# A third projection tile opened beside the first two behind a norm, in other PSUM banks, with its weights' low part on GpSimd

## The chip, the cores and the metric

One NeuronCore of a Trainium2 chip runs the whole kernel. The metric is the device time of one execution in microseconds (us). A program of 1 core has one span; lower is better.

## What is computed

Two layers of a backbone for 512 latent tokens and 256 context tokens of width 1024. Each layer is a token mixer and a gated feed-forward; here layer 0 mixes with a gated linear recurrence and layer 1 with windowed attention. Cut to what matters for this change:

```python
for i in range(DEPTH):                         # 2 layers
    hl = modulate(rms_norm(xl, norm1_g[i]), sh1, sc1)      # latent tokens; hc for the context tokens
    oc, ol = mixer_i(hc, hl, ...)              # i = 0: hgrn2, i = 1: qkv projection, rotation, attention
    xl = xl + g1 * ol
    h = modulate(rms_norm(xl, norm2_g[i]), sh2, sc2)
    u, v = jnp.split(h @ w_up, 2, axis=-1)     # 2 x 2816 columns
    u = conv3x3_depthwise(u) + conv_b          # on the 8 x 64 grid (1 x 3 for the context tokens)
    xl = xl + g2 * ((gelu(u) * v) @ w_down)
return rms_norm(xl, final_norm_g)
```

In layer 0 the context tokens go the same way; in layer 1 they give keys and values alone.

## The kernel before, in words

**Layout.** Channels lie on the 128 partitions, tokens on the free axis: `X[128, 8, 768]`, eight chunks of 128 channels, with 256 context tokens (`CTX`) and 512 latent ones (`LAT`), 768 together (`TOK`).

**Tiles.** A tile is one block of 128 output channels of a weight matrix. Its 1024 x 128 weights stream through three buffers (`WR`, `NB = 3`), in one fixed order of tile numbers `t`. Every product is made of three fp32r matmuls: high weights by high input, high by low, low by high. ScalarE makes the high part (`WH`, `split_high`), VectorE the low part (`WL`, L1433, `split_low`), as `WR - WH`. The semaphore `w_hi_done` counts high parts, `w_split` low parts, `tile_done` finished tiles. SyncE loads tile t when `tile_done` has reached t - 2.

**PSUM.** There are four pairs of banks: `SLOT[0]` and `SLOT[1]` for tiles in turn, `MA` for sums and matmuls that only keep TensorE busy, and `MB` for other things (the spread row of the norm among them). `begin_tile(s)` waits for `w_split` and for `evacuated[s]`, which counts the tiles that were taken out of slot s.

**The norm and the first tiles.** Behind a norm (`norm_dve`, `norm_act`) the input arrives in eight chunks: VectorE multiplies X by the coefficients and the row in `MB` (`scaled`, L1570) into one of two buffers `NT`, ScalarE adds the shift and rounds to the high part `HH` (L1077), VectorE makes the low part `HL` (`low`, L1577, reads `NT` and `HH`) and raises `lo_ready`. `first_tiles` works on two tiles at once, one chunk behind the other: it waits for each chunk and does both tiles' matmuls of it (L447 to L449). After that `third_tile` and `full_tile` do one tile each (768 tokens: L458). Behind chunk 5 VectorE makes the low weights of the third tile.

**The first feed-forward.** Tiles are u0, v0, u1, v1, ...: an odd one of the pair is convolved, an even one is the gate. Tile 50 (`T_FF0`) is u0 in slot 0, tile 51 is v0 in slot 1, tile 52 is u1, tile 53 is v1. ScalarE copies u0 to the padded grid `UP` (L1266, L1268) and scales it into `ACC` (L1270), VectorE adds the other eight taps (L1859) and two for the context (L1855), and in between makes a tile's low weights; ScalarE does the Gelu (L1276), and VectorE multiplies by v0 in slot 1 (L1867), which frees slot 1 for v1.

**The attention's projections.** Tile 118 (`T_AT`) gives keys of all 768 tokens, the next four queries of the 512 latent ones, then values of all; then the same again. ScalarE copies each into `RAW` (L1348), VectorE rotates it (`rope_sums`, L1983 to L1987), and between `rope_sums` and `rope_low` it makes the low weights of the tile three ahead. `RAW` has two buffers, so from the third on ScalarE waits for `roped`.

**GpSimd.** It makes low parts of the heads' outputs at the end of layer 0's mixer (L393) and the low weights of tile 51 (L398). From then on it has nothing until the attention.

Of the kernel before, what the change touches and what calls it, by code (L numbers as in the profile page):

```python
# [29 lines left out]
KC = D // P  # L30
CTX, LAT = 256, 512
TOK = CTX + LAT
# [26 lines left out]
STEPS = T_FF1 + FF_TILES  # L59
TILES = STEPS - 2  # L60
EARLY = HEADS - 2
ADA_GROUPS = 24
ADA_FIRST = 4
ADA_ORDER = (0, 2, 1, 3)
# [42 lines left out]
def trunk(nc, small_in, x_in, ada_in, w_in, ident_in, masks_in, rope_in, rot_in, tri_in, out):  # L107
    ctx = ExitStack()
    with ctx:
# [277 lines left out]
        @block.gpsimd  # L387
        def _(pool):
            def split_heads():

                for h in range(HEADS - 1):
                    pool.wait_ge(early_hi, h + 1)
                    pool.tensor_tensor(HL[:, h, :], Y[:, h, :], HH[:, h, :].bitcast(F32), ALU.subtract).then_inc(early_lo, 1)  # L393

            def weights_low(t):

                pool.wait_ge(w_hi_done, t + 1)
                pool.tensor_tensor(WL[t % NB][:, :, :], WR[t % NB][:, :, :], WH[t % NB][:, :, :].bitcast(F32), ALU.subtract).then_inc(w_split, 1)  # L398

            split_heads()  # L400
            weights_low(T_FF0 + 1)

            def sink_columns():

                pool.wait_ge(nsink_ready, 1)
                for u in range(len(UNITS)):
                    i, bi, r, part = UNITS[u]
                    hd, n = i * 8 + part * 4 + r, chunks(u)
                    if u >= NPB:
                        pool.wait_ge(p_turned, u - NPB + 1)  # L410
                    pool.tensor_scalar(PB[u % NPB][:, n * P:n * P + 1], nsink[:, hd:hd + 1], 1.0, 0.0, ALU.mult, ALU.add).then_inc(sink_col, 1)
                    if u >= 3:
                        scaled_probs(u - 3)
                for u in range(len(UNITS) - 3, len(UNITS)):
                    scaled_probs(u)

            def scaled_probs(u):

                n = chunks(u) * P
                pool.wait_ge(rden_ready, u + 1)  # L420
                pool.tensor_scalar(PB[u % NPB][:, 0:n], PB[u % NPB][:, 0:n], rden[u % 4][:, :], 1.0, ALU.mult, ALU.mult).then_inc(probs_scaled, 1)

            pool.wait_ge(tile_done, T_AT + 12)
            sink_columns()

        @block.tensor
        def _(pe):
# [38 lines left out]
            def first_tiles(tokens, tokens1=None, hg=False):  # L466

                for s in range(2):
                    begin_tile(s)
                done = parts.now()  # L470
                parts.add(KC)
                for k in range(KC):
                    pe.wait_ge(lo_ready, done + k + 1)
                    for s in range(2):
                        for half in range(2) if (tokens, tokens1 or tokens)[s] == TOK else (1,):
                            products(s, half, k, HH, HL, hg=hg)

            def full_tile(s, tokens, hi, lo, kn=KC, hg=False):
                begin_tile(s)
# [338 lines left out]
            def feed_forward():  # L818
                gated.add(2)
                for g, n in enumerate(GROUPS):  # L820
                    if g == 0:
                        first_tiles(TOK)
                        third_tile(TOK)
                        full_tile(1, TOK, HH, HL)
                    ada_tiles(n // 2 - (g == 0), TOK, HH, HL)
                    gated.add(n)
                    begin_tile(0)
                    for k in range(n):
                        if k in (0, n - 1):
                            pe.wait_ge(g_lo, gated.now(k == 0))  # L830
                        for half in range(2):
                            products(0, half, k, GH, GL, n)
                    full_tile(1, TOK, GH, GL, n)
                    if g < 2:
                        ada_tiles(1, TOK, GH, GL, n)
                        more_tiles(1, TOK, GH, GL, n)
                    else:
                        more_tiles(KC // 2 - 1, TOK, GH, GL, n)
# [13 lines left out]

            def at_projections():

                first_tiles(TOK, LAT)
                third_tile(LAT)
                full_tile(1, LAT, HH, HL)
                full_tile(0, LAT, HH, HL)
                full_tile(1, TOK, HH, HL)
                full_tile(0, TOK, HH, HL)  # L860
                pe.wait_ge(evacuated[1], tile.half(1))
                value_turns(MB)
                for j in range(4):
                    full_tile((j + 1) % 2, LAT, HH, HL)
                full_tile(1, TOK, HH, HL)
# [137 lines left out]
        def _(act):  # L1003
# [251 lines left out]
            def feed_forward(tokens):  # L1255
                freed.add(2)

                def body(i, adds):
                    for b in range(2):
                        next_tile()  # L1260
                        act.wait_ge(g_lo, freed.now(1))
                        freed.add()
                        conv_n.add()
                        act.wait_ge(taps_ready, conv_n.now())
                        lat, cx = padded(UP[b])
                        go(lat[:, 1:1 + GRID_H, 1:1 + GRID_W], SLOT[0][:, PL0:PE0].rearrange("p (h w) -> p h w", w=GRID_W), ACT.Copy)  # L1266
                        if tokens == TOK:
                            go(cx[:, 1:1 + CTX], SLOT[0][:, PC0:PL0], ACT.Copy)  # L1268
                        t0 = TOK - tokens
                        go(ACC[b][:, t0:TOK], SLOT[0][:, PE0 - tokens:PE0], ACT.Identity, scale=cw[b][:, 4:5], bias=cw[b][:, 9:10]).then_inc(evacuated[0], 1)  # L1270
                        split_high(tile.now() + AHEAD)
                        tile.add()
                        if b == 1 and adds:
                            ada_copy()
                        act.wait_ge(conv_done, conv_n.now())
                        go(ACC[b][:, t0:TOK], ACC[b][:, t0:TOK], ACT.Gelu).then_inc(gelu_done, 1)  # L1276
                        act.wait_ge(evacuated[1], tile.half())
                        go(GH[:, i * 2 + b:i * 2 + b + 1, t0:TOK].rearrange("p o t -> p (o t)"), ACC[b][:, t0:TOK], ACT.Copy).then_inc(g_hi, 1)

                for g, n in enumerate(GROUPS):  # L1280
                    for i in range(n // 2):
                        body(i, int(i >= int(g == 0)))
                    if g == len(GROUPS) - 1:
                        tile.add(KC)
                        continue
                    skip_tiles(6)
                    ada_copy()
                    skip_tiles(2)
# [52 lines left out]
            def raw(s, j):  # L1341

                if j % 6 > 0:
                    next_tile()
                n = j - j // 6
                if n >= 2:
                    act.wait_ge(roped, n - 1)
                go(RAW[n % 2][:, :], SLOT[s][:, PL0:PE0], ACT.Identity, bias=bqkv[:, j:j + 1]).then_inc(evacuated[s], 1)  # L1348

            def rounded(i, j):  # L1350

# [67 lines left out]
        def _(dve):  # L1419
# [7 lines left out]
            def split_low(last):  # L1427
                while low.now() <= min(last, STEPS - 1):
                    t, k = low.now(), depth(low.now())
                    dve.wait_ge(w_hi_done, t + 1)  # L1430
                    if t == T_FF0 + 2:
                        dve.wait_ge(w_split, t)
                    tt(WL[t % NB][:, 0:k, :], WR[t % NB][:, 0:k, :], WH[t % NB][:, 0:k, :].bitcast(F32), ALU.subtract).then_inc(w_split, 1)  # L1433
                    low.add()
# [359 lines left out]
            def final_residual():  # L1794

                for c in range(KC):
                    if c < KC - 1:
                        dve.wait_ge(fin_done, c + 1)
                    else:
                        dve.wait_ge(tile_done, T_FF0)  # L1800
                    for po, to, v in spans(TOK):
                        last = stt(X[:, c, to], SLOT[c % 2][:, po], ada[:, G1 * KC + c, v:v + 1], X[:, c, to], ALU.mult, ALU.add)
                    if c < KC - 2:
                        last.then_inc(fin_added, 1)
                    else:
                        last.then_inc(evacuated[c % 2], 1)
                    if c > 0:
                        add_square(c - 1, TOK)
                    if c == 3:
                        split_low(T_FF0)  # L1810
                add_square(KC - 1, TOK)
                tile.add(2)
                low.add()

            first_norm()
            dve.wait_ge(masks_in_done, 16)
# [363 lines left out]
```

## Time and profile before

| | us |
|---|---|
| median of 3 executions | 1868.98 |
| lowest | 1867.51 |
| the profiled execution, its own time | 1872.3 |
| its span | 1870.5 |
| TensorE matmuls busy | 1795.4 (96% of the span) |
| VectorE busy | 1166.1 (62%) |
| ScalarE busy | 681.0 (36%) |
| GpSimd busy | 74.4 (4%) |

The mean granted clock of TensorE was 0.986 of full speed. Times in the rows are microseconds from the span's start; a row of a timeline gives the start, the duration, the engine, the line and the operands, and in brackets the idle time before it and what ended it. Several like instructions are merged in one row (x2); the duration is then from the first's start to the last's end. Ends of matmuls are modelled and overlap the next one's start.

### The profile page before, as it was taken

Reading aid. Unit: us, or ns where it says so; the run is one execution under the profiler, and the core shown is the slowest. Engines: PE = TensorE matmul, PEld = TensorE weight load, DVE = VectorE, ACT = ScalarE, POOL = GpSimd, SP = SyncE. Lnnn points to the kernel's source line nnn. Section 1 sums busy time; section 2 is a strip of 40 time slices with the busy share of each in tenths; the row PEclk is TensorE's granted clock in tenths of the full one; section 3 lists DMA queues with packets and bytes.
Section 4 is the critical chain, followed back from the end, with each engine's and each line's share of the span. In section 5 each row is a group of like instructions: output and inputs, shape, how many; then the busy total and the mean of one; then the engine's idle time right before and its main releaser. Section 6 shows DMA issues by size and latency. Waiting matters only on the chain.

```text
span 1870.5 us, 31522 instructions
## 1 busy us (share of the span) xinstructions
PE 1795.4 (96%) x13510; PEld 1532.8 (82%) x13510; DVE 1166.1 (62%) x1938; ACT 681.0 (36%) x1008; POOL 74.4 (4%) x140
## 2 busy tenths in 40 slices
PE   5999999999979999999999999999899999999997
PEld 4999999999868788888888888878655878888885
DVE  4467668676766876525664366576554598487485
ACT  4334433444322433212331133343775443233242
POOL 0000000000200000000000000000453000000000
PEclk9999999999989999999999999999999999999999
DMA  7221222222201133233323332222000222332323
GB/s 301 102 90 50 89 92 91 69 69 91 72 27 52 56 114 113 91 102 124 113 102 107 108 113 91 84 67 89 13 1 1 90 92 89 102 102 92 99 92 111
DMA packets 47882, 166.17 MB, mean 89 GB/s; under 512 B 4992, under 2 KB 7424, under 8 KB 47744
## 3 DMA queue, kind: packets, MB, share of 16 engines
q1 hardware_dynamic: 47744, 164.16, 25.6%
q8 instruction: 107, 1.75, 0.4%
q14 instruction: 31, 0.25, 0.0%
HBM read 162.05 MB, written 2.10 MB: 88 GB/s over the span
## 4 chain that ended last, share of the span: by engine, by line
PE 90%; DVE 6%; ACT 1%; issue 1%; DMA 1%; POOL 0%; DVEq 0%; SPq 0%; ACTq 0%
PE slot L458 31%; PE slot L447 9%; PE slot L449 8%; PE slot L448 8%; PE slot L960 4%; PE slot L962 4%; PE slot L961 4%; PE MB L515 3%; PE MA L619 2%; PE MA L961 2%; PE MA L962 2%; PE MA L960 2%; PE slot L913 2%; PE MB L880 1%; PE slot L890 1%
## 5 line engine op out<-in xcount | busy, mean ns | idle before, releaser
L1433 DVE TENSOR_TENSOR WL<-WR,WH 128x1024 fp32r<-128x1024 f32 (+1 forms) x205 | 248.5, 1213 | 216.0 <-ACT WH L1015 214.7
L1015 ACT ACTIVATE WH<-WR 128x1024 fp32r<-128x1024 f32 (+1 forms) x206 | 215.6, 1048 | 392.4 <-DMA WR<-in_w 392.3
L447 PE MATMUL slot<-HH,WH 128*128 128x384 f32 (+2 forms) x816 | 291.4, 357 | 10.5 <-DVE HL L1577 3.9
L449 PE MATMUL slot<-HH,WL 128*128 128x384 f32 (+2 forms) x816 | 281.8, 345 | 0.0
L448 PE MATMUL slot<-HL,WH 128*128 128x384 f32 (+2 forms) x816 | 281.7, 345 | 0.0
L458 PE MATMUL slot<-HH,WH 128*128 128x256 f32 (+1 forms) x816 | 216.4, 347 | 11.1 <-DVE X L1751 5.9
L458 PE MATMUL slot<-HH,WL 128*128 128x256 f32 (+1 forms) x816 | 212.0, 342 | 0.0
L458 PE MATMUL slot<-HL,WH 128*128 128x256 f32 (+1 forms) x816 | 209.7, 339 | 0.0
L458 PEld LDWEIGHTS slot<-HH,WH 128*128 128x128 f32 x816 | 151.9, 191 | 37.1 <-issue 15.6
L447 PEld LDWEIGHTS slot<-HH,WH 128*128 128x128 f32 x816 | 154.7, 190 | 29.4 <-issue 10.5
L458 PEld LDWEIGHTS slot<-HL,WH 128*128 128x128 f32 x816 | 155.5, 191 | 18.3
L458 PEld LDWEIGHTS slot<-HH,WL 128*128 128x128 f32 x816 | 154.9, 190 | 17.8
L449 PEld LDWEIGHTS slot<-HH,WL 128*128 128x128 f32 x816 | 154.2, 189 | 6.3
L448 PEld LDWEIGHTS slot<-HL,WH 128*128 128x128 f32 x816 | 154.5, 189 | 5.4
L1931 DVE SCALAR_TENSOR_TENSOR ACC<-UP,cw,ACC 128x512 f32<-128x512 f32 x176 | 132.0, 750 | 19.4 <-ACT ACC L1308 16.2
L1859 DVE SCALAR_TENSOR_TENSOR ACC<-UP,cw,ACC 128x512 f32<-128x512 f32 x176 | 131.9, 750 | 3.9
L960 PE MATMUL slot<-HH,WH 128*128 128x512 f32 x256 | 100.1, 391 | 0.8 <-DVE HL L1577 0.8
L962 PE MATMUL slot<-HH,WL 128*128 128x512 f32 x256 | 99.6, 389 | 0.0
L961 PE MATMUL slot<-HL,WH 128*128 128x512 f32 x256 | 99.6, 389 | 0.0
L458 PE MATMUL slot<-GH,WH 128*128 128x256 f32 (+1 forms) x308 | 79.1, 338 | 0.0
L458 PE MATMUL slot<-GL,WH 128*128 128x256 f32 (+1 forms) x308 | 78.4, 336 | 0.0
L458 PE MATMUL slot<-GH,WL 128*128 128x256 f32 (+1 forms) x308 | 78.4, 335 | 0.0
(243 smaller groups left out, 2995.2 us busy)
## 6 DMA issues: line engine op xcount, KB each, us to landing
WR<-in_w SPq DMA_DIRECT2D x198, 512.0 KB, 3.5
ada_raw<-in_ada SPq DMA_DIRECT2D x80, 512.0 KB, 4.6
AD<-in_ada SPq DMA_DIRECT2D x6, 1024.0 KB, 18.8
X<-in_x SPq DMA_DIRECT2D x4, 768.0 KB, 8.7
WR<-in_w SPq DMA_DIRECT2D x8, 384.0 KB, 3.0
ada_raw<-in_ada SPq DMA_DIRECT2D x2, 1024.0 KB, 13.7
out<-Y SPq DMA_DIRECT2D x8, 256.0 KB, 2.2
Y<-in_masks SPq DMA_DIRECT2D x1, 512.0 KB, 18.8
```

The costliest lines, as they stand in the source:

```text
L447: mm(SLOT[s][:, po], WH[w % NB][:, k, :], hi[:, k, to], start=(k == 0), stop=False)
L448: mm(SLOT[s][:, po], WH[w % NB][:, k, :], lo[:, k, to], start=False, stop=False)
L449: last = mm(SLOT[s][:, po], WL[w % NB][:, k, :], hi[:, k, to], start=False, stop=(k == kn - 1))
L458: last = mm(SLOT[s][:, po], wt[w % NB][:, k, :], x[:, k, to], start=(k == 0 and part == 0), stop=(k == kn - 1 and part == 2))
L515: last = mm(MB[32 * m:32 * m + 32, 0:P], silu_w[:, c, :], src(f)[:, m * P:(m + 1) * P], start=(c == 0), stop=(c == KC - 1))
L960: mm(dst, WH[w % NB][:, k, :], hi[:, k, t], start=(k == 0), stop=False)
L961: mm(dst, WH[w % NB][:, k, :], lo[:, k, t], start=False, stop=False)
L962: last = mm(dst, WL[w % NB][:, k, :], hi[:, k, t], start=False, stop=(k == kn - 1))
L1015: go(WH[t % NB][:, 0:depth(t), :], WR[t % NB][:, 0:depth(t), :], ACT.Copy).then_inc(w_hi_done, 1)
L1433: tt(WL[t % NB][:, 0:k, :], WR[t % NB][:, 0:k, :], WH[t % NB][:, 0:k, :].bitcast(F32), ALU.subtract).then_inc(w_split, 1)
L1859: ins = stt(acc, lat[:, dy:dy + GRID_H, dx:dx + GRID_W], cw[b][:, k:k + 1], acc, ALU.mult, ALU.add)
L1931: ins = stt(acc, grid[:, dy:dy + GRID_H, dx:dx + GRID_W], cw[b][:, k:k + 1], acc, ALU.mult, ALU.add)
```

## The change

Two places, the opening of the first feed-forward and that of the attention's projections, get `three_tiles` in the place of `first_tiles` and `third_tile`. The third tile goes to `MA` and not to slot 0. It starts when chunk 3 of the first two is done, and goes on with one chunk of its own (three chunks behind) after each chunk of theirs; its last four chunks follow at the end. It needs no wait for a slot, but waits for `w_split`. In the feed-forward ScalarE takes u1 from `MA`, and in the attention the second query tile. The low weights of tiles 52 and 120, which VectorE made behind chunk 5 of these norms, are made by GpSimd; as `w_split` counts in order, GpSimd waits for it before, and VectorE waits for GpSimd's before the next one. The counter `low` is now moved on inside `split_low`.

```diff
+POOL_LOWS = (T_FF0 + 1, T_FF0 + 2, T_AT + 2)
...
             def weights_low(t):
 
                 pool.wait_ge(w_hi_done, t + 1)
+                pool.wait_ge(w_split, t)
                 pool.tensor_tensor(WL[t % NB][:, :, :], WR[t % NB][:, :, :], WH[t % NB][:, :, :].bitcast(F32), ALU.subtract).then_inc(w_split, 1)
 
             split_heads()
-            weights_low(T_FF0 + 1)
+            for t in POOL_LOWS:
+                weights_low(t)
...
+            def three_tiles(tokens):
+
+                for s in range(2):
+                    begin_tile(s)
+                w, done = tile.now(), parts.now()
+                parts.add(KC)
+
+                def third(k):
+                    if k == 0:
+                        pe.wait_ge(w_split, w + 1)
+                    for part, (wt, x) in enumerate(((WH, HH), (WH, HL), (WL, HH))):
+                        for po, to, _ in spans(tokens[2]):
+                            last = mm(MA[:, po], wt[w % NB][:, k, :], x[:, k, to], start=(k == 0 and part == 0), stop=(k == KC - 1 and part == 2))
+                    if k == KC - 1:
+                        last.then_inc(tile_done, 1)
+
+                for k in range(KC):
+                    pe.wait_ge(lo_ready, done + k + 1)
+                    for s in range(2):
+                        for half in range(2) if tokens[s] == TOK else (1,):
+                            products(s, half, k, HH, HL)
+                    if k >= 3:
+                        third(k - 3)
+                for k in range(KC - 3, KC):
+                    third(k)
+                tile.add()
...
                     if g == 0:
-                        first_tiles(TOK)
-                        third_tile(TOK)
+                        three_tiles((TOK, TOK, TOK))
                         full_tile(1, TOK, HH, HL)
...
-                first_tiles(TOK, LAT)
-                third_tile(LAT)
+                three_tiles((TOK, LAT, LAT))
                 full_tile(1, LAT, HH, HL)
...
+                        u = MA if first and b == 1 else SLOT[0]
...
+                src = MA if j == 2 else SLOT[s]
+                go(RAW[n % 2][:, :], src[:, PL0:PE0], ACT.Identity, bias=bqkv[:, j:j + 1]).then_inc(evacuated[s], 1)
...
                     t, k = low.now(), depth(low.now())
+                    if t in POOL_LOWS:
+                        low.add()
+                        continue
                     dve.wait_ge(w_hi_done, t + 1)
-                    if t == T_FF0 + 2:
+                    if t - 1 in POOL_LOWS:
                         dve.wait_ge(w_split, t)
```

## Rows read from the trace of the kernel before

**Rows 1.** The page: share of the chain that ended last, by engine.
```profile
PE 90%; DVE 6%; ACT 1%; issue 1%; DMA 1%; POOL 0%; DVEq 0%; SPq 0%; ACTq 0%
```

**Rows 2.** Timeline of TensorE, first feed-forward; columns start, duration, instruction, idle before.
```profile
630.49 0.35 PE L447 MATMUL slot<-HH,WH 128*128 128x256 f32 x1 [0.26 <-DVE HL L1577]
...
637.10 0.39 PE L447 MATMUL slot<-HH,WH 128*128 128x256 f32 x1
...
644.81 0.39 PE L447 MATMUL slot<-HH,WH 128*128 128x256 f32 x1 [0.89 <-DVE HL L1577]
...
647.01 0.28 PE L447 MATMUL slot<-HH,WH 128*128 128x256 f32 x1
...
650.15 0.59 PE L458 MATMUL slot<-HH,WH 128*128 128x256 f32 x2 [0.89 <-ACT ACC L1270]
...
658.21 0.51 PE L458 MATMUL slot<-HH,WL 128*128 128x256 f32 x2
660.32 0.58 PE L458 MATMUL slot<-HH,WH 128*128 128x256 f32 x2 [1.60 <-DVE ACC L1867]
```

**Rows 3.** Timeline of VectorE, the same stretch.
```profile
631.43 1.14 DVE L1577 SCALAR_TENSOR_TENSOR HL<-Y,ada,HH 128x256 fp32r<-128x256 f32 x2
...
633.67 1.14 DVE L1577 SCALAR_TENSOR_TENSOR HL<-Y,ada,HH 128x256 fp32r<-128x256 f32 x2
...
641.42 1.22 DVE L1433 TENSOR_TENSOR WL<-WR,WH 128x1024 fp32r<-128x1024 f32 x1
...
659.22 0.95 DVE L1867 TENSOR_TENSOR ACC<-ACC,slot 128x768 f32<-128x768 f32 x1 [0.91 <-ACT ACC L1276]
```

**Rows 4.** Timeline of ScalarE, the same stretch.
```profile
630.12 1.04 ACT L1015 ACTIVATE WH<-WR 128x1024 fp32r<-128x1024 f32 x1
...
648.25 0.60 ACT L1266 ACTIVATE UP<-slot 128x512 f32<-128x512 f32 x1 [3.40 <-PE slot L449]
```

**Rows 5.** Timeline of GpSimd, end of layer 0's mixer and the first feed-forward.
```profile
500.89 3.62 POOL L393 TENSOR_TENSOR HL<-Y,HH 128x768 fp32r<-128x768 f32 x2 [500.45 <-ACT HH L1146]
...
625.81 2.35 POOL L398 TENSOR_TENSOR WL<-WR,WH 128x1024 fp32r<-128x1024 f32 x1 [73.42 <-ACT WH L1015]
```

**Rows 6.** Timeline of VectorE, beside these GpSimd instructions.
```profile
500.97 1.85 DVE L1673 TENSOR_TENSOR FD<-FD 128x6 f32<-128x6 f32 x2
...
626.87 2.19 DVE L1570 SCALAR_TENSOR_TENSOR Y<-X,coef,MB 128x256 f32<-128x256 f32 x4 [1.78 <-PE MB L555]
```

**Rows 7.** All instructions of line 1673: shortest, median and longest in ns.
```profile
L1673 DVE TENSOR_TENSOR FD<-FD x112: 157/243/1896, 106.3 to 575.1; 128x384 f32<-128x384 f32 x16, 128x192 f32<-128x192 f32 x16, 128x96 f32<-128x96 f32 x16, 128x48 f32<-128x48 f32 x16
```

**Rows 8.** Timeline of TensorE, behind two waits elsewhere.
```profile
47.64 0.69 PE L447 MATMUL slot<-HH,WH 128*128 128x384 f32 x1 [2.69 <-DVE HL L1525]
...
541.05 0.98 PE L458 MATMUL slot<-HH,WH 128*128 128x256 f32 x2 [5.89 <-DVE X L1751]
...
545.62 0.52 PE L458 MATMUL slot<-HL,WH 128*128 128x256 f32 x2
```

**Rows 9.** Busy time by stretch: window, length, engines, granted clock, DMA share, GB/s.
```profile
541.00:543.00 2.00, 1.95 (x6) 1.79 (x7) 1.89 (x4) 0.00 (x0) 0.00 (x0) 0.50 0.00 0
```

**Rows 10.** Timeline of TensorE, opening of the attention's projections.
```profile
1238.13 0.39 PE L447 MATMUL slot<-HH,WH 128*128 128x256 f32 x1 [0.25 <-DVE HL L1577]
...
1247.69 0.28 PE L447 MATMUL slot<-HH,WH 128*128 128x256 f32 x1
...
1250.13 0.47 PE L447 MATMUL slot<-HH,WH 128*128 128x512 f32 x1 [0.54 <-ACT RAW L1348]
...
1255.69 0.39 PE L447 MATMUL slot<-HH,WH 128*128 128x512 f32 x1
```

**Rows 11.** Timeline of VectorE, the same stretch.
```profile
1232.46 1.15 DVE L1577 SCALAR_TENSOR_TENSOR HL<-Y,ada,HH 128x256 fp32r<-128x256 f32 x2
...
1253.65 1.22 DVE L1433 TENSOR_TENSOR WL<-WR,WH 128x1024 fp32r<-128x1024 f32 x1
```

**Rows 12.** Timeline of ScalarE, the same stretch.
```profile
1231.14 1.04 ACT L1015 ACTIVATE WH<-WR 128x1024 fp32r<-128x1024 f32 x1
```

More of the change, by code:

```diff
@@ L1256, in feed_forward, with body @@
                 freed.add(2)
-                def body(i, adds):
+                def body(i, adds, first=False):
                     for b in range(2):
+                        u = MA if first and b == 1 else SLOT[0]
                         next_tile()
@@ L1265, in body @@
                         lat, cx = padded(UP[b])
-                        go(lat[:, 1:1 + GRID_H, 1:1 + GRID_W], SLOT[0][:, PL0:PE0].rearrange("p (h w) -> p h w", w=GRID_W), ACT.Copy)
+                        go(lat[:, 1:1 + GRID_H, 1:1 + GRID_W], u[:, PL0:PE0].rearrange("p (h w) -> p h w", w=GRID_W), ACT.Copy)
                         if tokens == TOK:
-                            go(cx[:, 1:1 + CTX], SLOT[0][:, PC0:PL0], ACT.Copy)
+                            go(cx[:, 1:1 + CTX], u[:, PC0:PL0], ACT.Copy)
                         t0 = TOK - tokens
-                        go(ACC[b][:, t0:TOK], SLOT[0][:, PE0 - tokens:PE0], ACT.Identity, scale=cw[b][:, 4:5], bias=cw[b][:, 9:10]).then_inc(evacuated[0], 1)
+                        go(ACC[b][:, t0:TOK], u[:, PE0 - tokens:PE0], ACT.Identity, scale=cw[b][:, 4:5], bias=cw[b][:, 9:10]).then_inc(evacuated[0], 1)
                         split_high(tile.now() + AHEAD)
@@ L1281, in feed_forward @@
                     for i in range(n // 2):
-                        body(i, int(i >= int(g == 0)))
+                        body(i, int(i >= int(g == 0)), g == 0 and i == 0)
                     if g == len(GROUPS) - 1:
@@ L1347, in raw @@
                     act.wait_ge(roped, n - 1)
-                go(RAW[n % 2][:, :], SLOT[s][:, PL0:PE0], ACT.Identity, bias=bqkv[:, j:j + 1]).then_inc(evacuated[s], 1)
+                src = MA if j == 2 else SLOT[s]
+                go(RAW[n % 2][:, :], src[:, PL0:PE0], ACT.Identity, bias=bqkv[:, j:j + 1]).then_inc(evacuated[s], 1)
             def rounded(i, j):
@@ L1812, in final_residual @@
                 tile.add(2)
-                low.add()
             first_norm()
```

## The prediction

> **What bounds the kernel now.** I read the page first, for who sets the end: the chain that ended last runs on TensorE for 90% of the span [rows 1]. A saving must be TensorE time, and what the change does is decided by what TensorE waits for at the two places that it touches. So I read the TensorE timeline there next, then VectorE, ScalarE and GpSimd beside it.
>
> In the first feed-forward [rows 2] the first chunk starts at 630.49 and the fourth at 637.10. The reader is to see two things. First, chunks come every 2.2 us, and a chunk of two tiles is about 2.1 us of matmuls (one tile of eight chunks runs from 650.15 to 658.56, which is 8.4 us, 1.05 a chunk). So TensorE has next to no idle time between chunks here; the one gap is 0.89 us ahead of 644.81. Second, two waits stand behind: 0.89 us ahead of the third tile, for ScalarE to empty slot 0, and 1.60 us ahead of the fourth tile at 660.32. That second wait is for VectorE's gate product (L1867), which empties slot 1. VectorE gives chunks every 2.23 us (low parts at 631.43 and 633.67), spends 1.22 us on the third tile's weights at 641.42, and does the gate product at 659.22 [rows 3].
>
> **The fourth tile's wait.** The chain of this wait starts when the first tile (u0) is finished: ScalarE copies it from 648.25 [rows 4], VectorE does the taps, ScalarE the Gelu, VectorE the product, and the fourth tile starts at 660.32, 12.1 us after u0. The change alters nothing in that chain, only where it starts. So I time u0, not the third tile.
>
> **Feed-forward, without any collision.** From the fourth chunk on, a chunk of the third tile (1.05 us) is put behind each chunk of the two. Chunk 7 then starts at 637.10 + 0.1 (start after a wait) + 4 x (2.10 + 1.05) = 649.8 and not at 647.01 [rows 2]: u0 is finished 2.7 us later, and so is everything behind it. The third tile ends at 649.8 + 2.1 + 4 x 1.05 = 656.1, 2.5 us earlier than 658.56, but the fourth can't start before 660.32 + 2.7 = 663.0. What is gained at the third is lost in a longer wait of 6.9 us. The 1.22 us that VectorE saves is worth nothing: from chunk 3 on TensorE is behind VectorE. The bank change (MA for slot 0) takes away the 0.89 us wait, inside the same time. Plus 2.7.
>
> **The low part on GpSimd.** Tile 52's high part is rounded by ScalarE from 630.12 for 1.04 us, to 631.16 [rows 4]. GpSimd took 2.35 us for such a part of tile 51, beginning 0.07 us behind ScalarE's end [rows 5]. It would run from 631.23 to 633.6. The matmuls want it at about 639.3, so the latency is hidden, with 5 us to spare. The new wait on w_split stands at nobody's cost: behind it GpSimd has nothing until the attention. But VectorE wants to start the low part of chunk 1 at 631.43. What does it do beside GpSimd? Two rows bound it. The products of X and the spread row (L1570) at 626.87 took 2.19 us for four beside GpSimd's 625.81 to 628.16, the usual time: nothing lost, but they read one operand from SBUF and one from PSUM. A pair of tiny products FD<-FD (L1673) at 500.97 took 1.85 us beside GpSimd's subtraction that started at 500.89 [rows 6], where the shortest takes 157 ns and the median 243 [rows 7]: stopped until GpSimd was done, and both of its operands lie in SBUF. The low part (L1577) reads NT and HH, both in SBUF, so I take the second row: it stands still from 631.43 to 633.6, 2.15 us. The bounds are 0 and 2.35.
> The Trainium skill (SBUF — State Buffer, Who interferes with whom) says that a VectorE instruction with two SBUF inputs contends with a GpSimd instruction that reads SBUF, and that the one that comes second is fully blocked. By that rule the sum is the one with 2.15; by a reading of L1570 alone it is the one with 0. No row here shows L1577 itself beside GpSimd.
> All chunks behind come 2.15 later, so chunk 3 is at 639.25, u0 and the fourth tile are 2.7 + 2.15 = 4.8 us late (fourth tile at 665.1, third ended at 658.2).
>
> **The clock.** TensorE then stands still for about 6.9 us. The nearest row is the wait of 5.89 us that ended at 541.05 [rows 8]: until 545.62 seven pairs of matmuls came every 0.64 us instead of 0.35, with the granted clock at 0.50, the 1.2 GHz level [rows 9]. That is 4.57 us for 2.45 us of work, 2.1 us lost. Its bounds are 1.3 (47.64, after a wait of 2.69: nine matmuls at 0.32 instead of 0.17) and 3. The tile's work is on the path, so I add 2.1.
>
> **Attention.** Here the pair is a 768-token and a 512-token tile: 1.75 us a chunk against 2.23, so there is a gap of some 0.4 us in each. The third adds 0.70. Chunk 3 starts at 1238.13, chunk 7 at 1247.69, the third tile at 1250.13, and the fourth (tile 121) at 1255.69 with no wait [rows 10]. Without a collision chunk 7 starts at 1238.13 + 0.1 + 4 x 2.45 = 1248.0, 0.3 later, and the third ends at 1248.0 + 1.75 + 2.8 = 1252.6, 3.1 us earlier. But tile 121's weights are loaded into the buffer that tile 118 frees at chunk 7, then rounded, then VectorE makes their low part from 1253.65, behind the first rotation [rows 11]. It ends at 1254.8 now, 1255.1 after: tile 121 starts at 1255.2, 0.5 earlier. The late thing is no more the third tile but the fourth's low part. With the collision (ScalarE's rounding of tile 120 ends at 1232.18 [rows 12], VectorE wants its second low part at 1232.46) all is 2.1 later: tile 121 starts at 1257.3, 1.6 us after its old time, behind a wait of some 2.6 us. The tiles that follow have their low parts 1 us or more ahead. Plus 1.6.
>
> **Sum.** 4.8 + 2.1 + 1.6 = +8.5 us on the span of 1870.5, so 1879.0. The profiled run took 1872.3, 3.3 over the median of 1868.98, so I carry the difference over to the median: 1877.5.
>
> **The rivals.**
> - No collision between VectorE and GpSimd (the row of L1570 holds): 2.7 + 2.1 - 0.5 = +4.3, 1873.3. Against it is the row at 500.97.
> - More drops of the clock. Three new waits of 2.1 to 2.6 us arise (chunk 1 at both places, tile 121). The 2.69 us ahead of 47.64 was followed by the low level, the 1.60 ahead of 660.32 was not. Each drop costs 1.3 us: with all three 8.5 + 4 = 12.5, 1881.5, with one 1878.8.
> - Faster: the gate product is not what holds the fourth tile. If slot 1 were free by 656.1, the fourth tile would start 4.2 us earlier than now, TensorE would not cool, and with -0.5 in the attention the time is 1864.3. It decides if the product ends before 656; it ends at 660.17 now, and its chain starts with u0, which comes later. The row names L1867 as the releaser, so I give it little.
>
> **Chances.** Forecast 0.52, no collision 0.17, more drops 0.22, faster 0.04, something unread 0.05. The likeliest gives 1877.5. The range reaches from 1872 (below it lie the faster case and the lower third of the case with no collision, with a spread of about 2 us between runs) to 1883 (three drops and some spread). A measurement of this kernel tells a change of over 2%, 37 us, from none. No case comes near it on either side: within 2% 0.98, 0.01 each beyond.
>
> **What would show it.** Right: on the timeline of the first feed-forward the first L1577 pair of chunk 1 takes over 3 us beside a GpSimd subtraction; TensorE has a wait of some 2 us ahead of chunk 1; the fourth tile starts 4 to 5 us later than 660.3 behind a wait of 6 to 7 us, with L1867 as the releaser, and its first matmuls run at a granted clock of 0.50; tile 121 waits for L1433. Wrong: L1577 keeps 1.14 us a pair (then the second rival), the fourth tile follows the third without a wait (the faster one), or the third tile waits for GpSimd's low part, which would mean that it took over 7 us.

## The result, and the profile after

| | before | after |
|---|---|---|
| median of 4 executions | 1870.11 us | 1879.91 us |
| ratio, 95% interval | | 1.005 [1.0037, 1.0062] |
| span of the profiled execution | 1870.5 us | 1879.0 us |

The change costs about 9 us, 0.5%. The interval of the ratio leaves out 1, and the change is far within the 2% that count as the same. One of the four executions before took 3543.0 us; the other three took 1867.5, 1869.0 and 1871.2 us. Forecast were 1877.5 (1872 to 1883) and a span of 1879.0.

The kernel after has other line numbers: low parts `HL` are L1610 (L1577 before), products with X L1603 (L1570), the gate product L1899 (L1867), low weights L1466 on VectorE (L1433) and L400 on GpSimd (L398), the two first tiles L450 to L452 (L447 to L449), the third L493, a whole tile L461 (L458).

Timeline of TensorE after, first feed-forward: start, duration, instruction, idle before. They answer to [rows 2].
```profile
633.31 0.39 PE L450 MATMUL slot<-HH,WH 128*128 128x256 f32 x1 [1.79 <-DVE HL L1610]
...
633.88 0.63 PE L450 MATMUL slot<-HH,WH 128*128 128x512 f32 x1
...
657.79 0.51 PE L493 MATMUL MA<-HH,WL 128*128 128x256 f32 x2
665.12 0.98 PE L461 MATMUL slot<-HH,WH 128*128 128x256 f32 x2 [6.82 <-DVE ACC L1899]
665.89 0.84 PE L461 MATMUL slot<-HL,WH 128*128 128x256 f32 x2
...
671.01 0.59 PE L461 MATMUL slot<-HH,WH 128*128 128x256 f32 x2
```
Timeline of VectorE after, the same stretch ([rows 3]).
```profile
625.56 2.19 DVE L1603 SCALAR_TENSOR_TENSOR Y<-X,coef,MB 128x256 f32<-128x256 f32 x4 [0.96 <-PE MB L585]
...
627.89 1.15 DVE L1610 SCALAR_TENSOR_TENSOR HL<-Y,ada,HH 128x256 fp32r<-128x256 f32 x2
...
630.13 3.12 DVE L1610 SCALAR_TENSOR_TENSOR HL<-Y,ada,HH 128x256 fp32r<-128x256 f32 x2
...
634.35 1.14 DVE L1610 SCALAR_TENSOR_TENSOR HL<-Y,ada,HH 128x256 fp32r<-128x256 f32 x2
...
664.02 0.95 DVE L1899 TENSOR_TENSOR ACC<-ACC,slot 128x768 f32<-128x768 f32 x1 [0.91 <-ACT ACC L1305]
```
Timeline of GpSimd after ([rows 5]), and of ScalarE when it takes the first tile ([rows 4]).
```profile
625.33 2.37 POOL L400 TENSOR_TENSOR WL<-WR,WH 128x1024 fp32r<-128x1024 f32 x1 [73.25 <-ACT WH L1043]
629.93 2.38 POOL L400 TENSOR_TENSOR WL<-WR,WH 128x1024 fp32r<-128x1024 f32 x1 [2.24 <-ACT WH L1043]
```
```profile
653.05 0.60 ACT L1295 ACTIVATE UP<-slot 128x512 f32<-128x512 f32 x1 [8.53 <-PE slot L452]
```
Busy time by stretch after: window, length, TensorE, weight loads, VectorE, ScalarE, GpSimd, granted clock, DMA share, GB/s ([rows 9]).
```profile
666.00:668.00 2.00, 2.00 (x8) 1.71 (x7) 2.00 (x2) 2.00 (x4) 0.00 (x0) 0.50 0.00 0
```
Timeline of TensorE after, the attention's fourth tile ([rows 10]).
```profile
1263.52 0.50 PE L450 MATMUL slot<-HH,WH 128*128 128x512 f32 x1 [2.58 <-DVE WL L1466]
```

What to see: GpSimd's subtraction at 629.93 runs 2.38 us to 632.31, and the low part of chunk 1, which starts at 630.13, ends at 633.25 after 3.12 us instead of 1.14. TensorE waits 1.79 us for it. The third tile ends at 658.30 and is followed by 6.82 us of nothing, until the gate product has emptied slot 1. Nine pairs of matmuls then come every 0.65 us instead of 0.35, at a granted clock of 0.50, the 1.2 GHz level.

Four marks split each profile: the first low part of the feed-forward (A), the last square of the next norm (B), the first low part of the attention (C), the copy of its second value tile (D). Before, A is at 629.20, B 1221.28, C 1230.22, D 1314.75. A stretch of unaltered code can agree with before to 0.01 us (A to B in the run of the attention alone) or differ by 1 us with the clock (B to C).

| stretch, against before (us) | after | after, again | feed-forward only | attention only | lows on GpSimd only | MA only | lows on VectorE | gate copied | filler 15 | MA and copy |
|---|---|---|---|---|---|---|---|---|---|---|
| A to B, feed-forward | +8.83 | +8.54 | +6.37 | 0.01 | +1.47 | -0.37 | +5.56 | +1.49 | +4.45 | -2.79 |
| B to C, the norm | -1.11 | -1.11 | -0.43 | -0.43 | -1.10 | -0.44 | -0.43 | -1.10 | -1.11 | -1.11 |
| C to D, projections | +1.56 | +1.53 | -0.03 | +2.36 | +0.89 | -0.67 | +2.27 | +1.53 | +1.53 | -0.69 |
| timed ratio | 1.005 | 1.0049 | 1.0041 | 1.0019 | 1.0009 | 0.9995 | 1.0042 | 1.0027 | 1.0039 | 0.998 |

### The profile page after: what moved, and what is told of

It reads as the page before. It is cut to its first block, busy times and chain, and to the rows that moved or that the text cites. A ratio compares the mean times of both kernels' runs of the same rounds, so it can differ in the third digit from the quotient of the medians.

```text
span 1879.0 us, 31522 instructions
## 1 busy us (share of the span) xinstructions
PE 1793.9 (95%) x13510; PEld 1533.2 (82%) x13510; DVE 1167.7 (62%) x1936; ACT 681.6 (36%) x1008; POOL 79.2 (4%) x142
## 4 chain that ended last, share of the span: by engine, by line
PE 90%; DVE 6%; ACT 2%; issue 1%; DMA 1%; POOL 0%; DVEq 0%; SPq 0%; ACTq 0%
PE slot L461 31%; PE slot L450 9%; PE slot L452 8%; PE slot L451 8%; PE slot L988 4%; PE slot L990 4%; PE slot L989 4%; PE MB L545 3%; PE MA L649 2%; PE MA L988 2%; PE MA L990 2%; PE MA L989 2%; PE slot L941 2%; PE MB L908 1%; PE slot L918 1%
## 5 line engine op out<-in xcount | busy, mean ns | idle before, releaser
L1466 DVE TENSOR_TENSOR WL<-WR,WH 128x1024 fp32r<-128x1024 f32 (+1 forms) x203 | 246.0, 1213 | 216.1 <-ACT WH L1043 215.0
L450 PE MATMUL slot<-HH,WH 128*128 128x384 f32 (+2 forms) x808 | 288.5, 357 | 16.0 <-DVE HL L1610 5.6
L452 PE MATMUL slot<-HH,WL 128*128 128x384 f32 (+2 forms) x808 | 280.1, 347 | 0.0
L461 PE MATMUL slot<-HH,WH 128*128 128x256 f32 (+1 forms) x800 | 213.1, 349 | 15.4 <-DVE ACC L1899 6.8
L461 PE MATMUL slot<-HH,WL 128*128 128x256 f32 (+1 forms) x800 | 208.6, 343 | 0.0
L461 PE MATMUL slot<-HL,WH 128*128 128x256 f32 (+1 forms) x800 | 206.1, 340 | 0.0
L461 PEld LDWEIGHTS slot<-HH,WH 128*128 128x128 f32 x800 | 149.5, 192 | 40.8 <-issue 19.5
L450 PEld LDWEIGHTS slot<-HH,WH 128*128 128x128 f32 x808 | 153.9, 190 | 31.8 <-issue 10.0
L461 PEld LDWEIGHTS slot<-HL,WH 128*128 128x128 f32 x800 | 152.9, 191 | 18.3
L461 PEld LDWEIGHTS slot<-HH,WL 128*128 128x128 f32 x800 | 152.4, 191 | 17.4
L452 PEld LDWEIGHTS slot<-HH,WL 128*128 128x128 f32 x808 | 153.5, 190 | 6.1
L461 PE MATMUL slot<-GH,WH 128*128 128x256 f32 (+1 forms) x308 | 79.1, 338 | 0.0
L461 PE MATMUL slot<-GL,WH 128*128 128x256 f32 (+1 forms) x308 | 78.4, 336 | 0.0
L461 PE MATMUL slot<-GH,WL 128*128 128x256 f32 (+1 forms) x308 | 78.3, 335 | 0.0
```

The costliest lines, as they stand in the source:

```text
L450: mm(SLOT[s][:, po], WH[w % NB][:, k, :], hi[:, k, to], start=(k == 0), stop=False)
L452: last = mm(SLOT[s][:, po], WL[w % NB][:, k, :], hi[:, k, to], start=False, stop=(k == kn - 1))
L461: last = mm(SLOT[s][:, po], wt[w % NB][:, k, :], x[:, k, to], start=(k == 0 and part == 0), stop=(k == kn - 1 and part == 2))
```

## The experiments

The theory is the forecast's: (1) while GpSimd subtracts, VectorE's low part stands still; (2) the first tile ends later, and the fourth waits for the chain that starts with it; (3) the clock falls behind that wait; (4) in the attention the fourth tile waits for its own low weights. Rivals: the opening itself is the price, or the collision is all of it, or the clock is of no weight.

Every diff below is against the changed kernel, and cut (`...`). Where microseconds stand behind a ratio, they are the ratio times the median of before; the printed medians differ by up to 1 us more or less.

**GpSimd's low weights alone.** The kernel before with `POOL_LOWS` and nothing else.
```diff
-                        three_tiles((TOK, TOK, TOK))
+                        first_tiles(TOK)
+                        third_tile(TOK)
...
-                three_tiles((TOK, LAT, LAT))
+                first_tiles(TOK, LAT)
+                third_tile(LAT)
...
```


> The kernel before, with the low weights of tiles 52 and 120 on GpSimd and nothing else changed (no third tile beside the first two, no change of banks). Theory (VectorE's low part of chunk 1 stands still while GpSimd subtracts): the pair of chunk 1 takes 3.1 us instead of 1.14 at both places, all later chunks come 2.0 us later, the 1.2 us that VectorE saves behind chunk 5 gives part of it back, so the first tile ends 1.0 us later at each place: +2 us in all. Rival (the move to GpSimd is harmless or a gain): 1.14 us a pair, and the gap ahead of chunk 6 goes away at both places: -2 us.

Measured: 1872.75 us against 1871.1, ratio 1.0009 [1.0, 1.0018]. The timeline of VectorE, and of GpSimd beside it, in this run:
```profile
630.27 3.13 DVE L1612 SCALAR_TENSOR_TENSOR HL<-Y,ada,HH 128x256 fp32r<-128x256 f32 x2
```
```profile
630.07 2.38 POOL L400 TENSOR_TENSOR WL<-WR,WH 128x1024 fp32r<-128x1024 f32 x1 [2.24 <-ACT WH L1045]
```
The pair takes 3.13 us with no third tile in sight, at both places (the second at 1231.66, 3.13 too). It is the collision, 1.99 us each. A to B and C to D are 1.47 and 0.89 longer, where 1.0 each was expected. In the feed-forward this profile also has a fall of the clock behind the wait for chunk 1 (six matmuls of 512 columns from 634.03 take up to 0.63 us instead of 0.40), in the attention it has none. The rival's -2 is out.

**The third tile beside the first two, with the low weights on VectorE.**
```diff
-POOL_LOWS = (T_FF0 + 1, T_FF0 + 2, T_AT + 2)
+POOL_LOWS = (T_FF0 + 1,)
...
-                    if c == 5:
+                    if c == (2 if tokens == TOK else 5):
                         split_low(tile.now() + AHEAD)
```


> The changed kernel with the low weights of tiles 52 and 120 back on VectorE, but behind chunk 2, so that the third tile can start in time (GpSimd keeps tile 51). Theory (most of the loss is that the first tile ends later and with it the gate product that frees slot 1): no pair of 3.1 us, chunks from the third on come 1.2 us later instead of 2.0; the fourth tile still waits 6 to 7 us for the gate product and starts at half the clock: +7.5 us against before, 1 to 2 less than the changed kernel. Rival (the collision on VectorE is the main price): +2 us or less.

Measured: 1878.23 against 1871.1, ratio 1.0042 [1.0029, 1.0056], about +7.9 us. All of line 1610, shortest, median and longest in ns, first in the kernel after, then here:
```profile
L1610 DVE SCALAR_TENSOR_TENSOR HL<-Y,ada,HH x40: 477/744/2464, 627.9 to 1508.4; 128x512 fp32r<-128x512 f32 x24, 128x256 fp32r<-128x256 f32 x16
```
```profile
L1610 DVE SCALAR_TENSOR_TENSOR HL<-Y,ada,HH x40: 477/746/752, 631.1 to 1508.3; 128x512 fp32r<-128x512 f32 x24, 128x256 fp32r<-128x256 f32 x16
```
And TensorE's fourth tile here:
```profile
666.11 0.98 PE L461 MATMUL slot<-HH,WH 128*128 128x256 f32 x2 [6.81 <-DVE ACC L1899]
```
The collision is gone and most of the loss stays: 34.96 us from A to the fourth tile, against 31.12 before, behind the same wait of 6.8. The collision is not the main price. Of the 3.3 us that A to B is shorter than in the changed kernel, 2.3 are the earlier fourth tile; 1.0 comes behind it, where six pairs run at the low clock here and nine there. In the attention the fourth tile starts 26.03 us behind C, 0.86 earlier than in the changed kernel (26.89), but behind its wait the clock fell, which gave that back and more. TensorE, and the granted clock there:
```profile
1263.33 0.50 PE L450 MATMUL slot<-HH,WH 128*128 128x512 f32 x1 [2.74 <-DVE WL L1466]
```
```profile
1264.00:1266.00 2.00, 2.00 (x6) 1.61 (x5) 1.93 (x4) 0.66 (x1) 0.00 (x0) 0.50 0.04 14
```

**The slot emptied early.** The changed kernel, and one more copy on ScalarE.
```diff
+                        if first and b == 0:
+                            act.wait_ge(tile_done, tile.now() + 1)
+                            go(Y[:, 5, :], SLOT[1][:, PC0:PE0], ACT.Copy).then_inc(evacuated[1], 1)
...
-                        tt(ACC[b][:, t0:TOK], ACC[b][:, t0:TOK], SLOT[1][:, PE0 - tokens:PE0], ALU.mult).then_inc(evacuated[1], 1)
...
+                            tt(ACC[b][:, t0:TOK], ACC[b][:, t0:TOK], Y[:, 5, :], ALU.mult).then_inc(gated0, 1)
...
```


> The changed kernel with one more ScalarE copy (768 columns, about 0.9 us): the first gate tile goes from slot 1 to SBUF as soon as it is finished, slot 1 is free at once, and VectorE multiplies by the copy. Theory (the 6.8 us wait for slot 1 and the half clock behind it are the price in the feed-forward): the fourth tile now waits for its own low weights, which end at 660.0, so it starts some 5.0 us earlier, behind a wait of 1.8 us, and the clock does not fall: -5.0 - 2.9 = -7.9 us against the changed kernel, about +1 against before. Rival (the price lies in the opening itself): no change against the changed kernel, +8.5 against before.

TensorE's timeline here:
```profile
661.78 0.61 PE L461 MATMUL slot<-HH,WH 128*128 128x256 f32 x2 [1.83 <-DVE WL L1472]
...
680.39 0.59 PE L461 MATMUL slot<-HH,WH 128*128 128x256 f32 x2 [1.41 <-DVE ACC L1909]
```
The fourth tile waits 1.83 us for its low weights, as expected, and runs at full clock. From A to B the kernel is only 1.49 us above before, 7.3 below the changed kernel. Of these, 1.3 are not the copy's: ScalarE takes the first tile 23.87 us behind A here and 25.16 in the changed kernel, as the clock did not fall behind chunk 1. The other 6.0 are: the wait and its clock were the main price in the feed-forward. The 7.9 expected were not reached, since the second gate tile now waits 1.41 us: its convolutions start no earlier. The timed gain is smaller than the profile's: 1875.25 against 1871.1, ratio 1.0027 [1.0017, 1.0037], +5 us where the stretches from A to D say +1.9. A lies at 630.82 here against 629.20, and it varies over 3 us between profiles; what makes the rest of the difference is left open.

**Each place alone.** `three_tiles` and the low weights in one place, the other as before.
```diff
-POOL_LOWS = (T_FF0 + 1, T_FF0 + 2, T_AT + 2)
+POOL_LOWS = (T_FF0 + 1, T_FF0 + 2)
...
-                three_tiles((TOK, LAT, LAT))
+                first_tiles(TOK, LAT)
+                third_tile(LAT)
...
```


> The change in the feed-forward alone; the attention opens as before. Theory (two separate prices): +7 us against before. Rival (the attention's part is larger than read): +4 or less.

Measured: 1878.53 against 1870.63, ratio 1.0041 [1.0027, 1.0055], +7.7 us. TensorE:
```profile
664.72 0.98 PE L461 MATMUL slot<-HH,WH 128*128 128x256 f32 x2 [6.81 <-DVE ACC L1900]
```
From A to there it is 35.93 us against 31.12: 4.81 later, and the sum said 4.8. In the changed kernel it is 37.23, for a reason that the next section gives.

The second run has the change in the attention alone, by the same edit at the other place.

> The change in the attention's projections alone; the feed-forward opens as before. Theory: +1.5 us against before, with tile 121 behind a wait of about 2.6 us for its low weights (L1433 of before). Rival: no loss there (0 or a gain of 0.5), so that all 8.5 come from the feed-forward.

Measured: 1873.28 against 1870.63, ratio 1.0019 [1.001, 1.0028], +3.6 us, more than the 1.5 expected; +2.36 in its stretch. TensorE's fourth tile, and the granted clock behind its chunk 1:
```profile
1259.39 0.50 PE L450 MATMUL slot<-HH,WH 128*128 128x512 f32 x1 [2.88 <-DVE WL L1467]
```
```profile
1238.00:1240.00 2.00, 2.00 (x6) 1.53 (x5) 1.97 (x5) 1.12 (x2) 0.00 (x0) 0.50 0.00 0
```
Both places lose, and 7.7 and 3.6 add up to somewhat more than the 9.4 of both together, which their intervals allow. The attention's 0.8 beyond the 1.56 of the changed kernel goes with that drop of the clock behind the wait for chunk 1.

**The banks alone.** The third tile in MA, all its chunks behind the first two, low weights on VectorE behind chunk 5.
```diff
-            def three_tiles(tokens):
+            def three_tiles(tokens, lag=3):
...
-                        three_tiles((TOK, TOK, TOK))
+                        three_tiles((TOK, TOK, TOK), KC)
...
```


> The change of banks alone: the third tile in MA at both places, but behind the first two as before, its low weights on VectorE behind chunk 5. Theory (the fourth tile is held by the gate product, whose chain starts with the first tile): in the feed-forward the third tile starts and ends 0.9 us earlier, the fourth starts where it did, behind a wait of 2.5 us: 0; in the attention the fourth tile comes 0.5 us earlier: -0.5 us in all, not to be told from none. Rival (the slot 0 wait was on the path): -1.4 us.

Measured: 1869.32 against 1870.63, ratio 0.9995 [0.9986, 1.0004]. TensorE:
```profile
659.04 0.59 PE L461 MATMUL slot<-HH,WH 128*128 128x256 f32 x2 [2.58 <-DVE ACC L1899]
```
From A to the fourth tile 31.13 us, before 31.12: the 0.9 us gained at the third tile became a wait of 2.58 instead of 1.60. The third tile's earlier start is worth nothing to the fourth. A to B is 0.37 us shorter all the same; that arises behind the fourth tile, and what makes it is left open. In the attention 0.67 us are gained.

**The clock.** The changed kernel with matmuls that fill the wait.
```diff
+                        for _ in range(28):
+                            mm(MB[:, 640:896], ident[:, :], small[:, 0:256], start=True, stop=True)
                         full_tile(1, TOK, HH, HL)
```


> The changed kernel with 28 matmuls of 256 columns into unused columns of MB between the third and the fourth tile, to fill the 6.8 us wait (they take about 6.2 us by the 0.22 us of the like ones in the norm). The result is not touched. Theory (the wait costs more than itself, since the clock falls behind it): the fourth tile starts at the same time but at full clock: -2.8 us against the changed kernel, +6 against before. Rival (the clock is of no weight): no change against the changed kernel.

Measured: 1883.21 against 1870.63, ratio 1.007 [1.0055, 1.0086], worse. TensorE:
```profile
657.29 12.25 PE L854 MATMUL MB<-small,ident 128*128 128x256 f32 x56
669.18 0.70 PE L461 MATMUL slot<-HH,WH 128*128 128x256 f32 x2
```
That run tested something else: the rows count 56 for 28 matmuls. A plain fp32 one stands in the trace as two instructions of 0.22 us, so the filler was twice as long as meant and delayed the tile: it starts 40.86 us behind A instead of 37.23, and A to B is 9.47 us above before. With 15 of them (`range(15)`), beside the changed kernel once more:

> As the run with 28 filling matmuls, but with 15: each of them is done in two passes of 0.22 us, so 28 took 12.25 us and ended 4 to 5 us behind the release of slot 1; 15 take 6.6 us and end with it. Theory (the clock falls behind the 6.8 us wait, which costs 2 to 3 us): the fourth tile starts at its old time at full clock, -2.8 us against the changed kernel, +6 against before. Rival (the clock is of no weight): no change against the changed kernel.

> The changed kernel once more, on the chip of the next run, to compare with it: 1.005 of before as the first time.

Measured on one chip against 1871.46: the changed kernel 1880.45, ratio 1.0049 [1.0034, 1.0064]; with the filler 1878.29, ratio 1.0039 [1.0025, 1.0053]. TensorE with the filler:
```profile
658.72 6.64 PE L854 MATMUL MB<-small,ident 128*128 128x256 f32 x30
665.69 0.59 PE L461 MATMUL slot<-HH,WH 128*128 128x256 f32 x2 [0.33 <-DVE ACC L1901]
666.12 0.51 PE L461 MATMUL slot<-HL,WH 128*128 128x256 f32 x2
```
The tile is released by the same gate product, but its pairs come every 0.35 us from the start. It starts 35.95 us behind A, as in the run of the feed-forward alone (35.93): the filler delays nothing. A to B is 4.1 us shorter than in the repeat of the changed kernel; 1.3 of that come before the filler, where the clock did not fall behind chunk 1, and 2.8 are the filler's. The two timed medians differ by 2.2, and as their intervals overlap, the times alone would not prove it.

**A version that beats both.** The order of before with two edits of the above: the third tile in MA (`lag` of `KC`), and the first gate tile copied out of slot 1.

> The order of before (third tile behind the first two, low weights on VectorE behind chunk 5), but the third tile in MA at both places and the first gate tile copied to SBUF by ScalarE. Theory: the third tile starts 0.9 us (feed-forward) and 0.5 us (attention) earlier, as it waits for no slot; the fourth tile follows it without a wait at 657.7 instead of 660.3; -2.6 and -0.5, together -3.1 us against before. Rival (the next gate tile takes over the wait, since VectorE's convolutions come no earlier): 0 to -1 us.

Measured: 1866.76 against 1871.1, ratio 0.998 [0.9971, 0.9989], -3.7 us. TensorE at the seam of the third and fourth tiles, with no idle time in brackets:
```profile
657.84 0.52 PE L493 MATMUL MA<-HH,WL 128*128 128x256 f32 x2
658.20 0.51 PE L461 MATMUL slot<-HH,WH 128*128 128x256 f32 x2
```
From A to the fourth tile 28.40 us against 31.12, 2.7 saved where 2.6 was expected, and 0.69 in the attention. The change of banks alone gave the fourth tile nothing, so the copy is needed; the copy without the change of banks was not run. No later gate tile waits: the first tile ends here when it did before, so the convolutions are on time.

## Why the prediction was right

**Which tile to time: right.** "So I time u0, not the third tile" carried the forecast. ScalarE takes the first tile 25.16 us behind A instead of 19.05, and the fourth tile starts 12.07 us behind that, as before (12.07).

**The collision: right.** 2.15 us was taken, 1.98 measured (3.12 - 1.14), twice, and seen alone in the run of GpSimd's low weights. The trace of before had it only for tiny products FD<-FD [rows 6, 7]; now L1610 itself shows it. The rule of the Trainium skill (SBUF — State Buffer, Who interferes with whom) holds here: with two operands in SBUF the pair did not end until 0.94 us after GpSimd was done (632.31), and L1603, with one operand in PSUM, took 2.19 us for four beside GpSimd's subtraction from 625.33 to 627.70, as in the kernel before.

**u0 and the fourth tile 4.8 us late: right where the clock holds, 1.3 too small in the changed kernel.** Where TensorE's clock holds, the lateness is 4.81 (the run of the feed-forward alone). Its two terms were off by a little in opposite directions: 2.7 for the opening, which by its own sum is 2.8 (649.8 - 647.01) and measured 2.83 (4.81 - 1.98), and 2.15 for the collision. In the changed kernel the lateness is 6.11. The clock fell once more, behind the 1.79 us wait for chunk 1: the matmul at 633.88 took 0.63 us instead of 0.40. That is one drop of the rival with more drops, at the 1.3 us that it gave to each; the forecast's sum had none.

Against it stands a low stretch that this profile lacks: before, the clock was low while the norm's row was spread, and the first low part came later. TensorE before, then after:
```profile
625.34 1.49 PE L555 MATMUL MB<-ident,rstd 128*128 128x128 f32 x6
```
```profile
624.65 0.87 PE L585 MATMUL MB<-ident,rstd 128*128 128x128 f32 x6
```
A is at 627.89 instead of 629.20, 1.31 earlier: 0.34 of that had arisen before the norm (its first filler matmul starts at 618.68 instead of 619.02), 0.97 in it. The second norm gained 1.11 in the same way. B to C, which no kernel here alters, takes 8.94 us before, 8.51 in five of the profiles and 7.83 in the others, so this is no effect of the change.

**The clock behind the long wait: right in kind, 0.7 too small in the changed kernel.** Forecast 2.1 us; from 665.12 to 671.01 nine pairs took 5.89 us for 3.13 us of work, 2.8 lost, and the repeat has nine in 5.90. Behind the same wait of 6.81 us six pairs took 3.76 us in the run of the feed-forward alone and 3.91 with the low weights on VectorE, for 2.09 us of work: 1.7 and 1.8 lost. The forecast lies between these sizes.

**Attention: right.** +1.6 forecast, +1.56 measured, with the fourth tile behind a wait of 2.58 us for L1466.

**The sum.** -1.31 to A, +8.83 to B, -1.11 to C, +1.56 to D, +0.53 to the end: +8.50. The feed-forward was forecast at 6.9 (4.8 + 2.1) and measured 8.83. That the span came out at 1879.0 exactly is luck in part: the terms that were too small (1.3 and 0.7 us) were offset by the norms' clock and the rest of the stretches outside, together -1.89, which were not in the sum. In the repeat the stretches outside are +0.68, -1.11 and -1.44, also -1.9 by chance, and its span is 1878.7. Of the rivals, no collision (1873.3) and the faster one (1864.3) are out. More drops came true in part: of the three new waits, the one for chunk 1 of the feed-forward was followed by the low clock, and the other two (2.13 and 2.58 us) were not. The timed median of 1879.91 lies between its cases of one drop and three (1878.8, 1881.5).

## What to carry to other kernels

Before starting a later piece of work earlier, find what the engine waits for behind it, and time the start of that chain: work slipped in ahead of the chain's first link delayed everything behind it here, though it kept the engine full. Where a PSUM slot is held for a slow consumer, one cheap copy on an idle engine can free it (0.82 us of ScalarE, L1302, for 2.7 us of TensorE here, with the third tile in banks of its own). Before an instruction is moved to GpSimd, look whether VectorE has one with two SBUF operands at that time: here that cost 1.98 us at each place.

## What the hardware showed beyond the expected

- The clock fell behind a wait of 1.79 us (633.31), where a wait of 1.60 us before did not do it [rows 2] and one of 2.13 us ahead of 1242.05 in the changed kernel did not either. Even the same wait of 1.79 or 1.80 us for chunk 1 of the feed-forward was followed by the low clock in three profiles (changed kernel, its repeat, GpSimd's lows alone) and not in four (feed-forward only, gate copied, both fillers); the one of 2.13 to 2.15 us in the attention was in two (attention only, the filler of 28) and not in five. The length of one wait does not decide it, and what does is left open. Profiles of kernels that are alike there so differ by 1.3 us in the feed-forward.
- A plain fp32 matmul of 256 columns counts as two instructions of 0.22 us each (56 for 28), where an fp32r one is one of 0.12 us (637.06 to 637.18 in the changed kernel).
- The stretch ahead of A differs by 3 us between profiles of kernels that are alike there (627.89 to 631.15), which is more than most effects told of here. The stretches between marks showed them, the total times alone would not.
